# One run of near and far products, and a forget gate over the whole array, in gated linear attention

## The reference, cut to what matters

```python
log_a = jax.nn.log_sigmoid((glr @ w_gate_up + b_gate)) / GLA_TAU   # glr: 16 wide
# per chunk, b = cumsum(log_a) over the tokens
o_inter = einsum('bhcd,bhde->bhce', qc * exp(b), state)
dec = exp(where(causal, b_i - b_j, -inf))
att = einsum('bhid,bhjd,bhijd->bhij', qc, kc, dec)
o_intra = einsum('bhij,bhje->bhie', att, vc)
new_state = exp(b_last) * state + einsum('bhcd,bhce->bhde', kc * exp(b_last - b), vc)
```

## Time and profile before

| | |
|---|---|
| median of 3 runs | 745.33 us (743.96 to 746.56) |
| profiled execution | 743.97 us |
| its span | 742.1 us |
| PE busy | 705.5 us (95%) |
| DVE, ACT, POOL busy | 355.3 (48%), 327.3 (44%), 75.6 (10%) us |
| the change's loop | about 279.9 to 376 us of the span |

### The profile page before, as it was taken

The page is one execution under the profiler, slowest core; times in us unless marked ns, Lnnn a source line. Parts: engine busy times, 40 slices in busy tenths (PEclk is TensorE's granted clock), DMA queues, the critical chain, the costliest instruction groups (busy, mean ns, idle before and its releaser), DMA issues.

```text
span 742.1 us, 16684 instructions
## 1 busy us (share of the span) xinstructions
PE 705.5 (95%) x7025; PEld 546.4 (74%) x7025; DVE 355.3 (48%) x782; ACT 327.3 (44%) x779; POOL 75.6 (10%) x113
## 2 busy tenths in 40 slices
PE   2799999999999999999999999999999999999995
PEld 1486878788789986777766666777677889678884
DVE  0454380030202025777675576667671111389977
ACT  1254651121212137667656566645675667602100
POOL 0000000000000010101111201132113443000000
PEclk9999999999999999999999999999999999999999
DMA  9995300303001011000010000202756774103332
GB/s 293 396 375 174 114 0 1 114 0 97 0 1 57 1 43 51 9 14 11 10 11 1 1 1 1 59 1 76 240 183 222 274 267 175 60 1 116 123 132 85
DMA packets 35301, 70.31 MB, mean 95 GB/s; under 512 B 6626, under 2 KB 17979, under 8 KB 33564
## 3 DMA queue, kind: packets, MB, share of 16 engines
q1 hardware_dynamic: 30602, 47.73, 19.8%
q0 software_dynamic: 4016, 20.97, 8.1%
q10 hardware_dynamic: 610, 0.55, 0.3%
HBM read 62.26 MB, written 6.07 MB: 92 GB/s over the span
## 4 chain that ended last, share of the span: by engine, by line
PE 90%; DVE 3%; SPq 2%; DMA 2%; ACT 1%; issue 1%; another core or an unknown queue 1%; DVEq 0%; ACTq 0%
PE banks L1988 21%; PE banks L2174 8%; PE banks L2000 6%; PE banks L2302 5%; PE banks L2383 4%; PE banks L2403 3%; PE banks L2152 3%; PE banks L2512 3%; PE banks L2514 3%; PE banks L2513 2%; PE banks L2090 2%; PE banks L2009 2%; PE banks L2452 2%; PE banks L2471 2%; PE banks L2495 2%; DMA s_x<-in_x_prompt 2%
## 5 line engine op out<-in xcount | busy, mean ns | idle before, releaser
L1044 ACT ACTIVATE s_z<-banks 128x512 f32<-128x512 f32 (+3 forms) x40 | 19.6, 501 | 130.0 <-PE banks L1988 130.0
L1988 PE MATMUL banks<-s_w_parts,s_h_b 128*128 128x272 f32 (+3 forms) x328 | 68.0, 323 | 0.0
L1253 ACT ACTIVATE s_z<-banks 128x512 f32<-128x512 f32 (+2 forms) x88 | 41.4, 517 | 47.1 <-PE banks L2383 46.3
L1417 DVE COPY s_zs<-banks 8x512 f32<-8x512 f32 (+3 forms) x6 | 3.5, 576 | 118.5 <-PE banks L1962 118.5
L1988 PEld LDWEIGHTS banks<-s_w_parts,s_h_b 128*128 128x128 f32 x328 | 49.3, 189 | 4.9 <-issue 1.7
L1244 ACT ACTIVATE s_z<-banks,s_temps 128x896 f32<-128x896 f32 (+7 forms) x64 | 47.2, 742 | 11.6 <-DVE s_temps L1712 8.6
L1988 PE MATMUL banks<-s_w_parts,s_h_a 128*128 128x256 f32 (+2 forms) x256 | 49.7, 314 | 0.0
L1988 PE MATMUL banks<-s_z_r,s_h_b 128*128 128x512 f32 (+1 forms) x152 | 48.8, 387 | 0.0
L2383 PEld LDWEIGHTS banks<-s_ident,s_z 128*128 128x128 f32 x288 | 33.3, 141 | 11.8 <-issue 5.5
L2383 PE MATMUL banks<-s_ident,s_z 128*128 128x128 f32 x288 | 39.8, 274 | 1.6 <-DVE s_z L1728 1.6
L1988 PE MATMUL banks<-s_z_r,s_h_a 128*128 128x512 f32 x128 | 40.9, 395 | 0.0
(11 more groups left out here) (391 smaller groups left out, 1520.7 us busy)
## 6 DMA issues: line engine op xcount, KB each, us to landing
s_z<-in_w_ada SPq DMA_DIRECT2D x16, 512.0 KB, 12.2
s_temps<-in_w_in SPq DMA_DIRECT2D x3, 2048.0 KB, 7.7
s_x<-in_x_prompt SPq DMA_DIRECT2D x8, 512.0 KB, 11.8
s_z<-in_w_ada SPq DMA_DIRECT2D x1, 4096.0 KB, 13.8
s_kt<-in_w_out SPq DMA_DIRECT2D x8, 512.0 KB
s_temps<-in_x_prompt SPq DMA_DIRECT2D x8, 512.0 KB
out_y_prompt<-s_temps SPq DMA_DIRECT2D x7, 512.0 KB
s_temps<-in_w_in SPq DMA_DIRECT2D x2, 832.0 KB, 14.2
```

What stands on the lines that cost most here:

```text
L1253: nc.scalar.activation(PTb[r % 3][:, 4 * g:4 * g + n, :], banks[:, 4 + (groups(r) + g) % 2, 0:P * n].rearrange("p (j q) -> p j q", j=n), A ...
L1988: last = nc.tensor.matmul(banks[:, proj_bank(c, t), 0:WIDTH[c]], h_[half][:, k, n0:n0 + P], w_, start=(k == 0 and n == 0), stop=(k == KT - ...
```

## The change

w_gu gets 128 rows, zero beyond row 16; the gate's transposes take 128 columns instead of 16 and the forget gate 128 rows. PE's near products come in one run with the far products behind them (their 32-column ones first), after decays 0 and 1 and before the latent keys. ScalarE takes decay 1 before `soft`, and the far blocks before the latent keys. VectorE takes `near_pairs` before `log_decay`.

```diff
--- before.py
+++ after.py
@@ -158,7 +158,7 @@
         F, F_parts, w_uq = in_turn(("front", [P, 2 * H * QK], F32), ("front_parts", [P, 2 * H * QK], F32R), ("w_uq", [P, 2, H * QK], F32))
         w_uk = sb("w_uk", [P, H * NOPE])
         w_uv = sb("w_uv", [P, H * VD])
-        w_gu = sb("w_gu", [GR + 1, GH * DK])
+        w_gu = sb("w_gu", [P, GH * DK])
         g_q = sb("g_q", [P, QR])
         g_kv = sb("g_kv", [P, KVR])
         b_gt = sb("b_gt", [P, GH * DK])
@@ -236,7 +236,7 @@
                       [z_r[:, t, L0:L0 + w0] for t in (0, 1, 2, 5, 6, 7)])
 
         taken[0] = 0
-        glT = carve(P, rows=GR + 1)
+        glT = carve(P)
         zneg = carve(256)
         zmin = carve(256)
         la = [carve(256) for _ in range(2)]
@@ -413,6 +413,7 @@
         uq_in = sem("uq_in")
         w_in_in = [sem(f"w_in_in{i}") for i in range(NCH)]
         padded = sem("padded")
+        gu_padded = sem("gu_padded")
         masks_ready = sem("masks_ready")
         chain_d = sem("chain_d")
         chain_a = sem("chain_a")
@@ -748,6 +749,7 @@
             sp.wait_ge(rest_in, 16)
             sp.wait_ge(modT_done, 2)
             sp.dma_start(ada_gate, w_ada[:, :, 2 * D:3 * D]).then_inc(rest_in, 16)
+            sp.wait_ge(gu_padded, 1)
             with nc.allow_non_contiguous_dma(reason="gains by column"):
                 for dst, src in CONSTS[1:]:
                     sp.dma_start(dst, src).then_inc(const_in, 16)
@@ -833,6 +835,7 @@
 
         @block.gpsimd
         def _(pool):
+            nc.gpsimd.memset(w_gu[:], 0.0).then_inc(gu_padded, 1)
             nc.gpsimd.memset(cT, 0.0).then_inc(padded, 1)
             nc.gpsimd.memset(hsT[:], 0.0).then_inc(padded, 1)
             nc.gpsimd.memset(eps_t[:], EPS).then_inc(padded, 1)
@@ -1175,14 +1178,12 @@
                 if 0 <= k + 1 < T:
                     latent_out(k + 1)
                     decay(k + 1, 0)
+                    decay(k + 1, 1)
                 if k + 2 < T:
                     n_a = soft(k + 2)
+                far_blocks(k)
                 if 0 <= k + 1 < T:
-                    decay(k + 1, 1)
                     latent_keys_out(k + 1)
-                if k >= 0:
-                    far_blocks(k)
-                if 0 <= k + 1 < T:
                     decay(k + 1, 2)
                     decay(k + 1, 3)
                     decay_rest(k + 1)
@@ -1586,10 +1587,10 @@
                     gate_out(k - 1)
                 if k + 2 < T:
                     n_d = gate_parts(k + 2)
+                near_pairs(k)
+                if k + 2 < T:
                     log_decay(k + 2)
-                if 0 <= k < T:
-                    near_pairs(k)
-                    near_blocks(k)
+                near_blocks(k)
                 if 0 <= k + 1 < T:
                     n_d = scaled(k + 1)
                 if k + 3 < T:
@@ -2036,7 +2037,7 @@
                     pe.wait_ge(la_ready, t)
                 if t > 1:
                     pe.wait_ge(e_ready, 5 * (t - 1))
-                nc.tensor.transpose(banks[0:GR, 7, 256:384], z[:, t, W_GL:W_GG], ident[:]).then_inc(gl_transposed, 1)
+                nc.tensor.transpose(banks[:, 7, 256:384], z[:, t, W_GL:W_GL + P], ident[:]).then_inc(gl_transposed, 1)
 
             def key_query_rows(t):
                 if t == 1:
@@ -2073,14 +2074,13 @@
                 nc.tensor.matmul(banks[:, 7, 0:256], after_r, la_hi[t % 2], start=True, stop=False)
                 nc.tensor.matmul(banks[:, 7, 0:256], after_r, la_lo[t % 2], start=False, stop=True).then_inc(cum_done, 1)
 
-            def near_products(t, levels):
-                if levels[0] == 0:
-                    pe.wait_ge(x_ready, t + 1)
-                    pe.wait_ge(v_copied, t + 1)
-                    if t > 0:
-                        pe.wait_ge(near_in, t)
-                        pe.wait_ge(S_ready, 2 * t)
-                for n in levels:
+            def near_products(t):
+                pe.wait_ge(x_ready, t + 1)
+                pe.wait_ge(v_copied, t + 1)
+                if t > 0:
+                    pe.wait_ge(near_in, t)
+                    pe.wait_ge(S_ready, 2 * t)
+                for n in range(LEVELS - WIDE + 1):
                     for hp in range(2):
                         for g in range(4):
                             for par in range(2):
@@ -2089,23 +2089,22 @@
                                 right = kq[t % 2][rows, 256 + c0:256 + c0 + 32] if n == 0 else left
                                 last = nc.tensor.matmul(banks[32 * g:32 * g + 32, 2 + par, 64 * n + 32 * hp:64 * n + 32 * hp + 32], left, right,
                                                         start=True, stop=True)
-                if levels[-1] == LEVELS - WIDE:
-                    last.then_inc(att_done, 1)
+                last.then_inc(att_done, 1)
 
             def far_products(t):
                 if t > 0:
                     pe.wait_ge(gated_ready, t)
                 for hp in range(2):
-                    for par in range(2):
-                        rows, c0 = slice(64 * par, 64 * par + 64), P * hp
-                        nc.tensor.matmul(banks[0:64, 4 + par, 256 + 64 * hp:320 + 64 * hp], xs[rows, 0, c0:c0 + 64], xs[rows, 0, c0 + 64:c0 + 128],
-                                         start=True, stop=True)
-                for hp in range(2):
                     for blk in range(2):
                         for par in range(2):
                             rows, c0, at = slice(64 * par, 64 * par + 64), P * hp + 64 * blk, 96 - 32 * blk
-                            last = nc.tensor.matmul(banks[at:at + 32, 4 + par, 256 + 32 * hp:288 + 32 * hp], xs[rows, 1, c0:c0 + 32],
-                                                    xs[rows, 1, c0 + 32:c0 + 64], start=True, stop=True)
+                            nc.tensor.matmul(banks[at:at + 32, 4 + par, 256 + 32 * hp:288 + 32 * hp], xs[rows, 1, c0:c0 + 32],
+                                             xs[rows, 1, c0 + 32:c0 + 64], start=True, stop=True)
+                for hp in range(2):
+                    for par in range(2):
+                        rows, c0 = slice(64 * par, 64 * par + 64), P * hp
+                        last = nc.tensor.matmul(banks[0:64, 4 + par, 256 + 64 * hp:320 + 64 * hp], xs[rows, 0, c0:c0 + 64], xs[rows, 0, c0 + 64:c0 + 128],
+                                                start=True, stop=True)
                 last.then_inc(far_done, 1)
 
             def outputs(t):
@@ -2254,20 +2253,15 @@
                     decays(k + 1, 0)
                 if k + 2 < T:
                     forget_gate(k + 2)
-                if 0 <= k < T:
-                    near_products(k, range(0, 2))
                 if 0 <= k + 1 < T:
                     decays(k + 1, 1)
-                if 0 <= k < T:
-                    near_products(k, range(2, 4))
+                near_products(k)
+                far_products(k)
                 if 0 <= k + 1 < T:
                     latent_keys(k + 1)
                 if k == T - 1:
                     for q in range(2):
                         q_transpose(0, q)
-                if 0 <= k < T:
-                    near_products(k, range(4, 6))
-                    far_products(k)
                 if 0 <= k + 1 < T:
                     decays(k + 1, 2)
                     decays(k + 1, 3)
```

## The result

The changed kernel takes **756.68 us** in the median of 4 runs (751.94 to 758.33), against 745.94 before: ratio 1.0137, 95% interval 1.0084 to 1.019. It is 1.4% slower, beyond the top of the range. Its profiled execution took 755.50 us (span 753.7).

What follows compares the result with a forecast made beforehand. PE, busy 95% of the span, was taken as the bound. Less PE work (-8.2 us), more instruction-fetch stalls (+8.2) and waits for key copies (+1.2) gave +1.2 us, 746.5 for the median, range 739 to 751.

Steps and rivals of the forecast that it cites:

- Stalls, 12.3 us against 4.1: PE's dense product run, steps 0 to 6: instruction fetch lags, seven stalls of 1.75 us, 8.2 us more than today.
- Rival A: Loop's instruction fetch stays where it is, saving arrives, ScalarE sets the floor: 739.3 us; chance 0.28 including what lies between.
- the saving on PE: Loop and prologue: fewer passes and changes of array form, 1.07 us per full step, 8.2 us less work.
- ScalarE's and VectorE's orders: At key_query_rows PE waits for ScalarE's late key copies, 0.2 us in six steps, 1.2 us; VectorE's order costs nothing.
- The far products: End of PE's run: 32-column products first, in the near products' form, take 0.13 instead of 0.26 us, saving 0.13.
- Forget gate: Forget gate over all rows, in loop and prologue: 0.63 becomes 0.43 us, saving 0.20 each.
- the decay ahead of it: Decay matmul before the forget gate no longer leaves its form of the array, saving 0.09 us.
- joins: Near products in one run: two joins per step, 0.15 us each, saving 0.30.
- the keys: Latent keys on PE are now followed by full-array work, saving 0.09 us a step.
- the wider gate rows: Gate rows over 128 columns on PE: between 0 and 0.07 us saved a step, taken as 0.05.
- Rival B: Near products, steps 0 to 6: whole fetch lag of 2.3 us paid at each boundary, 750.9 us; chance 0.23.
- Rival C: PE's form changes cost less: saving 5 instead of 8.2 us, stalls grow half as much, 745.6; chance 0.12.

Runs made afterwards that it cites:

- Experiment 9: Kernel before the change, with PE made to wait for a chain of eight GpSimd memsets ahead of the near products of tiles 0 to 6: 770.40 us, ratio 1.0313.
- experiment 7: Changed kernel's full-array gate and early decays, but keys between near groups 3 and 4, ScalarE and VectorE in old order: 745.92 us, 1.0006 of the kernel before.
- experiment 8: Kernel before the change with only the full-array gate and the 32-column far products first, all other orders as before: 743.31 us, ratio 0.9971.

## Why the prediction was wrong

- **Stalls, 12.3 us against 4.1: right**, in place, spacing and in the sum, and near in the distance from the packet (2.3 to 2.9 us, 2.3 to 2.5 forecast). That the sum is exact is luck: the seven run from 0.80 to 2.52, three of them outside the stated 1.5 to 2.4, and their mean is the 1.75. Rival A falls: a block that PE uses up in 1.1 us does not have its fetch hidden. The Trainium skill (Runtime: NRT & Kernel Launch, Instruction fetch mechanics) has the fetch of the next block mostly hidden; the stall of 1.94 us here is not.
- **The main failed step is the sum's silence on the clock.** It priced a stall at its own length and the clock at nothing. In the profiled execution PE had 1.2 GHz for 10.2 us of this loop, worth some 4; across the runs the clock is 3.2 of the loss. Experiment 9 shows that idle time does this with no long run in it. Which stall loses the clock stays open: the longest one did not. Two more terms were mis-sized, each by about 2 us: the saving on PE and ScalarE's and VectorE's orders.
- **The saving on PE was mis-sized:** 0.8 us a tile came in place of 1.07. The decay matmul behind the forget gate still takes 0.34 to the next start (333.68 to 334.02), though all around it is full-array, and the one behind the keys 0.31: these 0.10 to 0.11 are not paid for leaving a 64x32 form. In all these places float32 work stands in front of a float32r matmul; that this is what costs them is likely, but no run separates it. The far products took 0.61 (338.22 to 338.83), 0.02 less and not 0.13. Forget gate (0.20), the decay ahead of it (0.09) and joins (0.3) came as forecast, the keys gave 0.17 where 0.09 was forecast, and the wider gate rows gave nothing (0.05). In all about 6 us in place of 8.2. In whole runs the gate alone is worth 1.2, not 3.
- **ScalarE's and VectorE's orders: 0.2 us a tile forecast, some 0.45 came,** about 3 us in place of 1.2. `decays_after` starts right behind `log_decay`, `key_query_rows` right behind the key copies. The text called the first "about 8.0 against 8.1". That these orders are worth 8 us by themselves under PE's old order it did not see; in the changed kernel the stalls cover most of it.
- Sum of what was measured: -0.8 a tile and -0.8 ahead of the loop, about -6; +8.2 of stalls; +3 of waits; together +5, for 5.8 at equal clock; then 3.2 of clock make 9 of the 10.7. What is left is within what four runs can tell; how many dips of the clock an execution gets varies by itself (751.94 at a clock of 0.993, 758.33 at 0.981).
- Rival B had the sign but not the reason: its 2.3 us a tile came in two tiles of seven, the mean was 1.75. Rival C was right in its first half: the saving fell short, 6 us where it had 5, but the stalls grew by 8.2 and not by half of it.
- A tile in the middle of the loop has 557 of PE's records, not 552; the working had allowed for it (40 to 45).

## What to carry to other kernels

Count the instructions of a dense run before joining it, for a small float32 product is four of them here, two passes with a weight load each. Seven runs of 240 instructions had one stall, of 1.6 us; runs of 256 and 176 with only the keys between (experiment 7) had 9.1 us of stalls in seven tiles; runs of 432 lost 1.75 us on average, and then the clock. When PE's order moves, the orders of the engines that free its buffers have to move with it; here each half alone was slower than both together. Take the parts of a change that shorten work without lengthening a run, as in experiment 8.

## What the runs showed of the hardware that was not expected

From the start of a packet of 256 instructions to PE's resume it was 2.3 to 2.9 us in the changed kernel, and from PE's entry into the block at whose end it stood 2.8 to 3.8. A shift by 128 instructions alone moved a kernel by 9 us (two runs), 2.1 of them at equal clock. With PE idle 2.4 to 3.0 us in each of seven tiles the granted clock fell six times, for 27 us; with waits of 0.9 and 1.1 us a tile it did not fall in the loop.
